# Delta rule of a hybrid layer: chunk matrices stored by their 64x64 diagonal blocks, matrix products as pairs of quadrants, key rows ahead of the others

## The reference

```python
gc = cumsum(g) within a chunk                       # g <= 0, per head
decay = exp(gc[:, None] - gc[None, :])              # lower triangle
lmat  = strict_lower((k * beta) @ k.T * decay)      # 64 x 64 per head and chunk
tmat  = inverse(eye + lmat)
u, w  = tmat @ (v * beta), tmat @ (k * beta * exp(gc))
intra = lower(q @ k.T * decay)
for each chunk:                                     # the recurrence
    v_new = u - w @ state
    o     = (q * exp(gc)) @ state + intra @ v_new
    state = state * exp(g_last) + (k * exp(g_last - gc)).T @ v_new
out = rmsnorm(o) * silu(z)
```

## Time and profile before

| | |
|---|---|
| time, median of 3 runs | 2418.22 us (2415.72 to 2423.59) |
| profiled execution | 2406.9 us, span 2404.7 us |
| mean granted clock of TensorE | 0.927 |
| TensorE matmul busy | 2207.5 us (92%) |
| VectorE, ScalarE, GpSimd busy | 862.9, 739.6, 791.4 us |

### The profile page before, as it was taken

The page is one execution under the profiler, slowest core; times in us unless marked ns, Lnnn a source line. Parts: engine busy times, 40 slices in busy tenths (PEclk is TensorE's granted clock), DMA queues, the critical chain, the costliest instruction groups (busy, mean ns, idle before and its releaser), DMA issues.

```text
span 2404.7 us, 30222 instructions
## 1 busy us (share of the span) xinstructions
PE 2207.5 (92%) x13066; PEld 1906.3 (79%) x13066; DVE 862.9 (36%) x1290; ACT 739.6 (31%) x1085; POOL 791.4 (33%) x244
## 2 busy tenths in 40 slices
PE   7999999799888799999978999678778999999998
PEld 6898887688666699999976798577666888888886
DVE  3302771343576432112223155343443334320222
ACT  5432223355555432122324322200012223321222
POOL 4343224443213443343331033310111343444432
PEclk9999999899999899999988798678767999999999
DMA  4322212222111222332331011100000232223322
GB/s 152 103 91 88 67 65 98 79 71 88 53 36 36 70 88 75 92 97 75 97 76 36 1 62 53 36 1 1 1 1 18 92 101 88 92 84 105 105 65 76
DMA packets 167659, 163.16 MB, mean 68 GB/s; under 512 B 16604, under 2 KB 164440, under 8 KB 167528
## 3 DMA queue, kind: packets, MB, share of 16 engines
q1 hardware_dynamic: 166124, 159.02, 21.0%
q10 hardware_dynamic: 1404, 2.23, 0.3%
HBM read 159.14 MB, written 2.10 MB: 67 GB/s over the span
## 4 chain that ended last, share of the span: by engine, by line
PE 86%; DVE 5%; ACT 3%; issue 3%; POOL 1%; DMA 0%; ACTq 0%; DVEq 0%; SPq 0%; POOLq 0%
PE ps L1835 83%; PE ps L1837 3%; POOL residual L643 1%; POOL w_lo L620 1%; ACT diag L767 0%; ACT w_hi L739 0%; DVE gdn_nk L1675 0%; POOL stat L637 0%; DVE sumsq L1182 0%; ACT gdn_rows L1106 0%; DMA x_rows<-in_x 0%; DVE gdn_vn L1735 0%; DVE gdn_qg L1675 0%; DVE gdn_nq L1675 0%; DVE gdn_lt L1688 0%
## 5 line engine op out<-in xcount | busy, mean ns | idle before, releaser
L620 POOL TENSOR_TENSOR w_lo<-w_raw,w_hi 128x2048 fp32r<-128x2048 f32 (+3 forms) x157 | 676.6, 4312 | 947.1 <-ACT w_hi L739 947.1
L1835 PE MATMUL ps<-u_hi,w_hi 128*128 128x512 f32 (+1 forms) x1904 | 591.8, 351 | 32.0 <-DVE sg L1385 12.3
L1835 PE MATMUL ps<-u_lo,w_hi 128*128 128x512 f32 (+1 forms) x1904 | 583.1, 346 | 0.0
L1835 PE MATMUL ps<-u_hi,w_lo 128*128 128x512 f32 (+1 forms) x1904 | 581.2, 345 | 0.0
L1835 PEld LDWEIGHTS ps<-u_hi,w_hi 128*128 128x128 f32 x1904 | 335.2, 192 | 81.7 <-issue 16.8
L1835 PEld LDWEIGHTS ps<-u_hi,w_lo 128*128 128x128 f32 x1904 | 333.9, 192 | 43.2
L1835 PEld LDWEIGHTS ps<-u_lo,w_hi 128*128 128x128 f32 x1904 | 333.7, 192 | 40.7 <-issue 0.7
L739 ACT ACTIVATE w_hi<-w_raw 128x2048 fp32r<-128x2048 f32 (+3 forms) x157 | 279.8, 1783 | 179.4 <-PE ps L1835 164.6
L1835 PE MATMUL ps<-hidden_hi,w_hi 128*128 128x264 f32 (+1 forms) x528 | 141.1, 321 | 0.0
L1835 PE MATMUL ps<-hidden_lo,w_hi 128*128 128x264 f32 (+1 forms) x528 | 141.0, 322 | 0.0
L1835 PE MATMUL ps<-hidden_hi,w_lo 128*128 128x264 f32 (+1 forms) x528 | 140.8, 321 | 0.0
(11 more groups left out here) (362 smaller groups left out, 3326.0 us busy)
## 6 DMA issues: line engine op xcount, KB each, us to landing
w_raw<-in_w_in_a SPq DMA_DIRECT2D x23, 1024.0 KB, 5.3
w_raw<-in_ffn_w_gate SPq DMA_DIRECT2D x22, 1024.0 KB, 5.3
w_raw<-in_ffn_w_up SPq DMA_DIRECT2D x22, 1024.0 KB, 5.4
w_raw<-in_w_in SPq DMA_DIRECT2D x17, 1024.0 KB, 5.2
w_raw<-in_ffn_w_down SPq DMA_DIRECT2D x16, 768.0 KB, 4.2
w_raw<-in_ffn_w_down SPq DMA_DIRECT2D x16, 640.0 KB, 3.9
w_raw<-in_w_out_a SPq DMA_DIRECT2D x8, 1024.0 KB, 5.0
w_raw<-in_w_kv SPq DMA_DIRECT2D x8, 1024.0 KB, 5.3
```

The source lines that it names most:

```text
L620: pool.tensor_tensor(WL[:, u % RAWS, part], RAW[:, u % RAWS, part], WH[:, u % SPLITS, part].bitcast(F32), ALU.subtract).then_inc(lo_done, 1)
L1835: return nc.tensor.matmul(o, a, b, start=start, stop=stop, **kw)
```

## The change

- Matrices are stored by their diagonal blocks: 128 partitions x 8 heads x 64 columns, with chunk 0 in partitions 0 to 63 and chunk 1 in 64 to 127. The masks shrink with them (`chunk_masks`: two of 128 columns, seven of 64).
- Products on them are written as one product per chunk (`for r in chunks`): 64x64 weights in the quadrant of the array that belongs to partitions r and output partitions r. This holds for `kk`, `kq`, `d1` (now a product with the identity), `x`, `y` and `uw`. Both chunks' results go to one bank, save w and the scores.
- `decay` is one product of 512 columns, its exponential and the copy of `d1` one instruction of 512 columns each. `lt`, `at`, `e1a`, the evictions and subtractions of the levels work on half of the columns; `e1b` becomes one instruction per chunk.
- `turn_in` takes the key part first (`turn_in_k`), which no longer waits for `out_join`; `rows` is split the same way, and `kb`, `nk` wait for the key rows only. All rows together are now copied in three instructions.
- `turn_out` of a tile moves behind `kk` of the next, `out_gate` behind `e1b` of the next and `at` behind the first level. POOL's `kbg`, `kd`, `vb` wait for `e1b`; `ug` of the next tile waits for this tile's `decay` only. The exponential waits for `out_sum` of the tile before in place of `turn_out`.
- Banks 6 and 7 are no longer used by the stage. Several buffers (normed output, x, TI, UG) get a place of their own, and the waits that guarded their sharing go.

The diff, cut to its core (the step lists follow the new order; masks, placement and one-line renamings are left out):

```diff
                 if t:
-                    pool.wait_ge(g_pe, PE_AT[t - 1, ("x", levels(t - 1)[-1], 1)])
...
+                    pool.wait_ge(g_pe, PE_AT[t - 1, "decay"])
...
+                pool.wait_ge(g_dve, DVE_AT[t, "e1b"])
...
+                act.wait_ge(g_pe, PE_AT[t, "turn_in_k"])
+                nc.scalar.activation(ROWQ[0:w, 1, :], PS[0:w, 1, :], ACT.Copy).then_inc(g_act, one("act", t, "rows_k"))
                 act.wait_ge(g_pe, PE_AT[t, "turn_in"])
-                nc.scalar.activation(ROWQ[0:w, q0:3, :], PS[0:w, q0:3, :], ACT.Copy).then_inc(g_act, one("act", t, "rows"))
+                if t:
+                    nc.scalar.activation(ROWQ[0:w, 0, :], PS[0:w, 0, :], ACT.Copy)
+                nc.scalar.activation(ROWQ[0:w, 2, :], PS[0:w, 2, :], ACT.Copy).then_inc(g_act, one("act", t, "rows"))
...
                 if t > 1:
-                    act.wait_ge(g_pe, PE_AT[t - 1, "turn_out"])
...
+                    act.wait_ge(g_dve, DVE_AT[t - 1, "out_sum"])
+                nc.scalar.activation(DEC[0:w, :, 0:cw], PS[0:w, 0, 0:HEADS * cw].rearrange("p (h c) -> p h c", h=HEADS),
+                                     ACT.Exp).then_inc(g_act, one("act", t, "decay"))
...
+                    for a, bank in enumerate((2, 0)):
+                        nc.scalar.activation(WTT[:, :, 64 * a:64 * a + 64],
+                                             PS[:, bank, 0:4 * GDN_D].rearrange("p (h c) -> p h c", h=4), ACT.Copy)
...
+            def out_gate(t):
+                dve.wait_ge(g_pe, PE_AT[t, "turn_out"])
...
                 dve.wait_ge(g_dve, DVE_AT[t, "e1a"])
-                nc.vector.tensor_tensor(TIT[0:w, :, 0:w], IDENT[0:w, 0:w].unsqueeze(1).to_broadcast([w, HEADS, w]),
-                                        TIT[0:w, :, 0:w], ALU.subtract).then_inc(g_dve, one("dve", t, "e1b"))
-                if t:
-                    dve.wait_ge(g_pe, PE_AT[t, "kq"])
-                    for b in range(2):
-                        last = scores(AT, 3 + b, b, TRI[0:w, 0:1, 0:w].to_broadcast([w, 4, w]))
-                    last.then_inc(g_dve, one("dve", t, "at"))
+                for r in chunk_rows(t):
+                    last = nc.vector.tensor_tensor(TIT[r, :, 0:cw], IDENT[r, r].unsqueeze(1).to_broadcast([cw, HEADS, cw]),
+                                                   TIT[r, :, 0:cw], ALU.subtract)
+                last.then_inc(g_dve, one("dve", t, "e1b"))
+                if t > 1:
+                    out_gate(t - 1)
...
                     for g in range(2):
                         hs = slice(4 * g, 4 * g + 4)
                         dve.wait_ge(g_pe, PE_AT[t, ("x", s, g)])
-                        if n == 0:
-                            dve.wait_ge(g_pool, POOL_AT[t, "vb"])
-                            dve.wait_ge(g_dve, DVE_AT[t, "qg" if t else "nk"])
-                        nc.vector.tensor_tensor(XX[0:w, hs, 0:w], PS[0:w, g, 0:4 * w].rearrange("p (h c) -> p h c", h=4),
-                                                TRI[0:w, 3 + n:4 + n, 0:w].to_broadcast([w, 4, w]),
+                        nc.vector.tensor_tensor(XX[0:w, hs, 0:cw], PS[0:w, g, 0:4 * cw].rearrange("p (h c) -> p h c", h=4),
+                                                MASKS[0:w, 2 + n:3 + n, 0:cw].to_broadcast([w, 4, cw]),
                                                 ALU.mult).then_inc(g_dve, one("dve", t, ("x", s, g)))
                     for g in range(2):
...
-                            o = joined(dst[0:w, hs, 0:w], s, which)
-                            y = PS[0:w, bank, 0:2 * w].rearrange("p (h b s) -> p h b s", h=4, s=s)
+                            o = joined(dst[0:w, hs, 0:cw], s, which)
+                            y = PS[0:w, (3, 5)[g], first:first + 2 * cw].rearrange("p (h b s) -> p h b s", h=4, s=s)
                             nc.vector.tensor_tensor(o, o, y, ALU.subtract).then_inc(g_dve, one("dve", t, (name, s, g)))
+                    if t and n == 0:
+                        dve.wait_ge(g_pe, PE_AT[t, "kq"])
+                        for b in range(2):
+                            last = scores(AT, (4, 2)[b], b, MASKS[0:w, 0:1, 0:cw].to_broadcast([w, 4, cw]))
+                        last.then_inc(g_dve, one("dve", t, "at"))
...
-                for part in range(0 if t else 1, 3):
+                for part in (1, 0, 2) if t else (1, 2):
+                    if part == 0 and t > 1:
+                        pe.wait_ge(g_dve, DVE_AT[t - 1, "out_join"])
                     for c in range(4):
                         last = turn(PS[0:w, part, P * c:P * (c + 1)], CVS[:, 4 * part + c, cols], P)
-                last.then_inc(g_pe, one("pe", t, "turn_in"))
+                    if part != 0:
+                        last.then_inc(g_pe, one("pe", t, "turn_in_k" if part == 1 else "turn_in"))
...
-                for b in range(2):
...
+                mm(PS[0:w, 0, 0:HEADS * cw], BELOW[0:w, 0:w], UG[0:w, :, 0:cw]).then_inc(g_pe, one("pe", t, "decay"))
...
-                if t > 1:
-                    pe.wait_ge(g_dve, DVE_AT[t - 1, "out_gate"])
...
+                        d = slice(64 * (h % 2), 64 * (h % 2) + 64)
+                        for r in chunks:
+                            last = mm(PS[r, banks[h % 2], cw * (h // 2):cw * (h // 2 + 1)], KT[d, h // 2, r], x[d, h // 2, r])
...
+                if t > 1:
+                    turn_out(t - 1)
...
                 for h in range(HEADS):
-                    last = turn(PS[0:w, h // 4, w * (h % 4):w * (h % 4 + 1)], TIT[0:w, h, 0:w], w)
+                    for r in chunks:
+                        last = mm(PS[r, 0, cw * h:cw * (h + 1)], TIT[r, h, 0:cw], IDENT[r, r])
                 last.then_inc(g_pe, one("pe", t, "d1"))
                 for n, s in enumerate(levels(t)):
                     for g in range(2):
                         if n:
                             pe.wait_ge(g_dve, DVE_AT[t, ("d", levels(t)[n - 1], g)])
-                        else:
+                        elif g == 0:
                             pe.wait_ge(g_act, ACT_AT[t, "d1"])
-                            pe.wait_ge(g_dve, DVE_AT[t, "at" if t else "e1b"])
+                        elif t > 1:
+                            pe.wait_ge(g_dve, DVE_AT[t - 1, "out_gate"])
                         for h in range(4 * g, 4 * g + 4):
-                            last = mm(PS[0:w, g, w * (h % 4):w * (h % 4 + 1)], LT[0:w, h, 0:w], TI[0:w, h, 0:w])
+                            for r in chunks:
+                                last = mm(PS[r, g, cw * (h % 4):cw * (h % 4 + 1)], LT[r, h, 0:cw], TI[r, h, 0:cw])
                         last.then_inc(g_pe, one("pe", t, ("x", s, g)))
...
                             if s != levels(t)[-1]:
-                                mm(PS[0:w, (2, 7)[g], o], TIT[0:w, h, 0:w], joined(XX[0:w, h, 0:w], s, 0))
-                            last = mm(PS[0:w, 3 + g, o], XX[0:w, h, 0:w], joined(TIT[0:w, h, 0:w], s, 1))
+                                for r in chunks:
+                                    mm(PS[r, bank, o:o + cw // 2], TIT[r, h, 0:cw], joined(XX[r, h, 0:cw], s, 0))
+                            for r in chunks:
+                                last = mm(PS[r, bank, 256 + o:256 + o + cw // 2], XX[r, h, 0:cw], joined(TIT[r, h, 0:cw], s, 1))
                         last.then_inc(g_pe, one("pe", t, ("y", s, g)))
                 pe.wait_ge(g_dve, DVE_AT[t, ("e", levels(t)[-1], 1)])
+                pe.wait_ge(g_pool, POOL_AT[t, "vb"])
                 for h in range(HEADS):
...
-                    last = mm(PS[0:w, 5, hv], TIT[0:w, h, 0:w], ROWQ[0:w, 2, hv])
+                    d = slice(64 * (h % 2), 64 * (h % 2) + 64)
+                    for r in chunks:
+                        last = mm(PS[r, 4, hv], TIT[r, h, 0:cw], ROWQ[r, 2, hv])
                     if t:
-                        last = mm(PS[64 * (h % 2):64 * (h % 2) + 64, 6, P * (h // 2):P * (h // 2 + 1)], KBG[:, hv], TIT[:, h, :])
+                        for r in chunks:
+                            o = GDN_D * (h // 2)
+                            last = mm(PS[d, 2 if r.start == 0 else 0, o:o + cw], KBG[r, hv], TIT[r, h, 0:cw])
```

More of the change, by code:

```diff
@@ L434, in build @@
                 dve_steps += [(t, n) for n in ("kb", "nk")]
-            dve_steps += [(t, n) for n in ["turned_q"] * full + ["lt", "e1a", "e1b"] + ["at"] * full]
-            dve_steps += [(t, n) for s in levels(t) for n in [("x", s, 0), ("x", s, 1)]
-                          + [(kind, s, g) for g in range(2) for kind in ["d"] * (s != levels(t)[-1]) + ["e"]]]
+            dve_steps += [(t, n) for n in ["turned_q"] * full + ["lt", "e1a", "e1b"]]
+            dve_steps += [(t - 1, "out_gate")] * (t > 1)
+            for s in levels(t):
+                dve_steps += [(t, n) for n in [("x", s, 0), ("x", s, 1)]
+                              + [(kind, s, g) for g in range(2) for kind in ["d"] * (s != levels(t)[-1]) + ["e"]]]
+                dve_steps += [(t, "at")] * (full and s == levels(t)[0])
```

(33 more changed lines are left out.)

124 lines of the change are left out of this document (65 added, 59 removed).

## The result

The changed kernel takes 2301.3 us in the median of 5 runs, against 2418.1 for the kernel before, measured beside it. The forecast was 2352 with a range down to 2312, so the sign was right, but the time lies outside the range: the gain is 117 us against 66. One of the five runs took 4101.65 us, like no other here: without it the median is 2296.9, and the ratio of the two kernels, which leaves it out, is 0.948 (0.9415 to 0.9545).

The account below looks back on a forecast made before the run. TensorE (92% busy) was taken to bound the kernel, with the delta rule's 317.3 us going into the span one to one. Gains of 16.6, 12.9, 32.6 and 4 us made 66 off the 2418.2 median: 2352, range 2312 to 2378.

Parts of the forecast that it names:

- levels: Doubling levels of x and y products: 24.9 us per tile at the lower clock against 27.7 to 32.3; 16.6 us gained.
- `uw`: The u and w products behind the levels: 3.7 us per tile against 5.9 to 8.2; 13.3 us gained.
- recurrence: Chunk recurrence from `uw` to `out_join`: 0.4 us lost, since `ws` of t=1 would run at the lower clock.
- `out_join` to first x: Stretch from one tile's output end to the next tile's first doubling product: 15.9 us instead of 25.3; 32.6 gained together.
- one warm stretch per tile: Full clock once per tile over turn_q, kk or d1: 1 us gained in each, 4 in all.
- Which clock: Step on TensorE's clock: levels and `uw` with 64x64 products taken at 0.50 (1.2 GHz), one full-clock stretch per tile.
- The rival of full clock: Levels and `uw` all at full clock: 46 us more gained, 2306; warm in part or all, chance 0.16.
- Pair prices: Cost of 64x64 products in paired quadrants: 53 ns each at the lower clock, with bounds of 27 and 107 ns.
- the overlap: Paired row halves writing one bank overlap; the rival that they don't costs 109 us more, 2461 (slower: chance 0.10).
- keys first: Key turns ahead of `out_join`'s end: start at -1.5 us, done at -0.4, key rows by 1.2; part of the 32.6.
- GpSimd's wait: GpSimd held until `e1b` so VectorE's nk, nq, qg take 0.6 to 0.69 us, not 1.5; 6 us in all.
- The stage has no DMA that could carry this spread: Reason for taking the 66 us off the median 2418.2, 11 us above the profiled execution of 2406.9.

Follow-up runs that it names:

- e2: Changed kernel with all of chunk 0's x and y products of a group ahead of chunk 1's, instead of alternating; 2372.0 us, ratio 0.9823 to the kernel before.
- e4: Kernel before with all u products (128 weight columns) ahead of all w products (64) instead of taking turns; 2393.7 us, ratio 0.991 to the kernel before.
- e12: Changed kernel with idle TensorE waits filled by unread products, and all turns and rows waiting for `out_join` again; 2284.6 us, ratio 0.9463 to the kernel before.
- e11: Changed kernel's diagonal storage and quadrant pairs in the old kernel's order, with TensorE waits filled by unread products; 2304.2 us, ratio 0.9545 to the kernel before.
- e7: Changed kernel without GpSimd's wait for `e1b` ahead of `kbg`, `kd`, `vb`; 2296.6 us, ratio 0.9548 to the kernel before.
- e8: Kernel before, run again without edit for a second profile; 2412.8 us.
- e10: Changed kernel, run again without edit; 2296.0 us, ratio 0.9478 to the kernel before.
- e1: Changed kernel, run again without edit for its spread; 2270.5 us, ratio 0.9418 to the kernel before.
- e5: Changed kernel with unread whole-array products into bank 7 filling TensorE's waits to hold the clock; 2272.6 us, ratio 0.9441 to the kernel before.
- e9: Second run of the changed kernel with unread whole-array products filling TensorE's waits; 2275.6 us, ratio 0.941 to the kernel before.

## Why the prediction was wrong in size

Terms in us, from the first profile of each kernel:

| term | forecast | measured |
|---|---|---|
| levels | 16.6 | 44.3 (20.4, 20.2, 15.65, 15.65) |
| `uw` | 13.3 | 21.3 (1.7 in each tile) |
| recurrence, `uw` to `out_join` | -0.4 | 9.4 (9.7, 9.7, 12.3, 12.4 for 13.0 to 13.5) |
| `out_join` to first x | 32.6 | 41.3 (t=1 16.5, t=2 to 4 12.9, 11.4, 14.9; tile 0 2.0 gained) |
| one warm stretch per tile | 4 | in the terms above |
| sum | 66 | 116 |

- **The step that failed is "Which clock".** From 4.2 us of `state` and `out` products at 0.50 it concluded that products in quadrants of the array don't bring the full clock. In the trace, the levels' quadrant pairs of t=1 ran dense at 0.50 for 13.4 us and then the clock rose to 1.00, where whole-array products had been at 0.50 for 12.8 (in before's other tiles only for the first 3 to 4 us of the levels). In t=2 it was 13.1. Once risen at 1593.9 it stayed through `uw`, recurrence and turns to 1645.1. A row of 4.2 us couldn't tell what a longer dense stretch is granted. The Trainium skill's rule that was set beside it ("TensorE: Matmul & The Clock Gate", Why this matters for your kernels) says that continuous work gets the full clock; the trace agrees for pairs of quadrants. It doesn't for one quadrant at a time: in e2 34 us without a break stayed at 0.50, so the forecast's doubt about quarter-array work wasn't baseless. Nor does continuous work always keep the full clock: in the kernel before it fell at 1740.4, inside t=3's `uw`, after 26 us at 1.00 in which TensorE was busy for 25.5, and this `uw` took 8.21 us instead of 5.91. What decides isn't shown.
- **The rival of full clock was right in kind and came close in size** (112), in part by chance. Its 3.0 us a level and 2.0 for `uw` are the 3.07 and 1.7 of the warm stretches. Against its sum the levels gave 11.5 less (44.3 against 16.6 + 4 x 9.8 = 55.8, since two tiles ran partly cold), `uw` and the recurrence 11 more (30.7 against 12.9 + 4 x 1.7 = 19.7), the stretch to the first x 8.7 more, and its 4 for warm stretches is in these.
- **Pair prices, the level at 0.50, VectorE's and the y products' weight load** came out as forecast (53 ns, 5.15 us, no stall). e2 settles the overlap.
- **`uw`** was forecast at 3.7; it ran at 1.00 in all four tiles (the levels end so) in 1.7. The recurrence behind it ran at 1.00 in two. The size of the old `uw` was never explained; e4 shows it as switching of weights.
- **`out_join` to the first x** was forecast at 15.9 for a lower clock in the turns. Where the clock stayed up (t=3) it was 11.4; t=4, whose turns are cold (3.41 us), has 14.9, 1.0 under the forecast, as much as `kk` is below its 1.7. Of the reasons given, keys first holds (7 us with the waits filled). Output off the path and GpSimd's wait hold together with `at` (22), some 12 of it through GpSimd's wait. That this wait gives VectorE its 0.69 back is so where the rows come late: 684 ns in e12 with it, 1.53 us in e11 without. But the two overlap: with the key rows early (e7), kb, nk and nq are at 0.69 without the wait too, since they fit in while GpSimd is still at the output's power.
- **"The stage has no DMA that could carry this spread"**: right, but the medians carry another: the latent attention takes 86 to 114 us from one execution to the next, with the clock in it at 0.94 (first profile of the changed kernel) or 0.68 to 0.72 (before, e8, e10) over the same 80 us. What decides between them stays open. Three profiles have the short form, all with the changed stage (first, e1, e5); two others with it (e9, e10) have the longest, and those with before's stage take 105 to 114. The times of executions without a profile speak against a tie to the change: of the kernel before, four of eleven beside e5 took 2387 to 2393 us at a mean clock of 0.932 to 0.934, the others 2406 to 2421 at 0.919 to 0.928; beside e1 two of seventeen and beside e10 one of eleven lie as low. That is as much as the short form saves, though no profile of such an execution exists.

## What to carry to other kernels

Where a block-diagonal operand fills half of the array with zeros, write the blocks as products in opposite quadrants and issue them alternately: e2 against the changed kernel shows that the order alone is worth some 75 us, the clock that it brings included. Price each such edit at both clocks, and don't read from a burst of a few us which clock a new mix of products will get; a short row at the lower clock is no evidence. If a stage's waits let the clock fall, try products into a spare bank in those waits (worth 20 us here), and let weights of one shape stand together. Where two causes can hide each other, as GpSimd's wait and the early key rows do here, take each out in a kernel without the other as well.

## What the runs showed of the hardware beyond that

- Two row halves of the array wrote separate partitions of one bank at the same time: 52 ns per fp32 instruction of 64x64 at 0.50 and 29 at 1.00. Before's `ws`, whose row halves write two banks, took 25 at 1.00.
- Dense products in pairs of quadrants brought the clock from 0.50 to 1.00 after some 13 us (t=1, t=2; 17 in t=4 of e7); dense products in one quadrant at a time stayed at 0.50 for 34 us (e2).
- Products that alternate over all four quadrants (`kk`, two banks) took 0.62 us for 32, 19 ns each with the tail, at 1.00.
- Alternating weights of 128 and 64 columns cost 185 ns an instruction against 95 sorted (e4).
- VectorE and GpSimd slow each other to about 1.5 us for products of 512 columns from two SBUF operands (VectorE 1.53 for 0.69, GpSimd 1.55 for 1.04), in whichever instruction they meet; in e7 VectorE's copies out of PSUM (1647.96 and 1648.56) stayed at 0.68 beside GpSimd's kd, and kb to nq at 0.69 beside its power.
